# State-space stage of a two-block layer: turned rows in a bank of their own, first z product at the end of the projection

## The chip, the core and the metric

The kernel runs on one core of a Trainium2 chip. A core has a matrix engine (TensorE, PE in the rows; its weight loads are PEld), a vector engine (VectorE, DVE), a scalar engine (ScalarE, ACT), GpSimd (POOL), and SyncE (SP), which here only issues DMAs. Matmul results land in PSUM, eight banks of 128 partitions x 512 fp32. The metric is the device time of one execution in microseconds (us); lower is better, and the figure compared is the median of several runs.

## What is computed

Two transformer-like layers over 512 tokens of width 1024, all in fp32. The first has two branches on one modulated, normalised input `h`: sparse attention and a Mamba-2 state-space branch. The second has banded attention, a gated delta rule and a product-key expert layer. The change touches only the state-space branch, cut here to what matters:

```python
proj = h @ w_in                                   # z_ssm (2048), xbc (3072), dt_raw (32) among it
xbc = silu(causal_depthwise_conv(xbc, conv_w, conv_b))
xs, bm, cm = split(xbc, [2048, 2048 + 512])       # 32 heads of 64; 4 groups of B and C, state 128
dt = softplus(dt_raw + dt_bias); a = -exp(a_log)
y = ssd(xs, dt, a, bm, cm) + d_skip * xs          # chunked scan over 4 chunks of 128 tokens
y = y * silu(z_ssm)
y = rms_norm(y per group of 512 columns) * ssm_norm_g
y_ssm = y @ w_branch_ssm
```

## The kernel before

The program is a row of stages. Each opens a block in which every engine runs its own instruction list; a block ends in a meeting of all engines, so the next stage begins when the last of them is through. Inside a block engines order themselves by semaphores. `post` increments a semaphore and then makes the issuing engine wait for it.

Weights stream from DRAM through a ring of three 2 MB slots. `stream` (SP) issues the loads up to two chunks past the stage's last; `take` (TensorE) waits until a chunk is loaded.

**`ssm_projection_stage`.** TensorE makes 25 products of 8 matmuls (one for dt, 24 for the columns of xbc) into banks 0 to 7 in turn. For each, ScalarE scales and adds the bias (L1061), VectorE adds three further convolution taps (L1099, three instructions), and ScalarE applies silu (L1065, for the last one L1067). `pj.freed` counts banks given back by VectorE; product 23 is the last in bank 7, product 24 is in bank 0.

**`ssd_stage`.** The work is 16 units `n`: 4 groups `g` by 4 chunks `c`, one unit after the other. For each unit:

- `z_product(n)` (L1204): 128 tokens of `h` times 512 columns of the z weights, 8 matmuls of 128x512 in fp32, which the profile shows as 16 passes, into bank 7. ScalarE's `silu_z(n)` (L1284) reads bank 7.
- `front(n)`: TensorE turns the rows of xs and B (L1217, L1218) and multiplies C by B (L1219) into banks 0 and 1. ScalarE copies them out (L1291, L1295) and takes exponentials of the decays (L1297, L1298). VectorE takes the decays, which SP has spread over the partitions by a DMA from DRAM (L1188), and prepares and weights them (L1353 to L1366). GpSimd makes the skip term (L1417) and the decayed rows (L1421).
- `products(n)`: TensorE multiplies everything together (L1233 to L1239), banks 2, 3 and 6. Then GpSimd fades the state (L1428), VectorE updates it and sums the output rows (`sums`, L1377 to L1384), GpSimd multiplies by silu(z) (`gate`, L1433), ScalarE takes the root of the mean square (`root`, L1306 to L1308), and VectorE makes a diagonal matrix of it (`norm`, L1390).
- `turn_back(n)` (L1250): TensorE multiplies the rows of y by that diagonal, 4 matmuls of 128x128, 8 passes, which turns and normalises them, also into bank 7. ScalarE's `store(n)` (L1314) copies them out with the gain.

The order on each engine is written out by hand. On TensorE, iteration `n` is `front(n+1)`, `turn_back(n-2)`, `products(n)`, `z_product(n+2)`; the last two iterations have no z product, and two turn-backs stand behind the loop. On ScalarE it is `front(n+1)`, `store(n-2)`, `root(n-1)`, `silu_z(n+2)`. On VectorE it is `front(n+1)`, `sums(n)`, `norm(n-1)`.

Bank 7 is shared. So `z_product(n)` waits for `silu_z(n-1)` and `store(n-4)`, and `turn_back(n)` waits for `silu_z(n+3)` beside its own `norm(n)` and `store(n-1)`. Before the loop, TensorE turns dt and its cumulative sums into bank 4 (L1255, L1256), from which ScalarE copies three small tiles (L1321 to L1323); TensorE waits for these before `z_product(0)`, and nothing else uses bank 4.

`ssm_out_stage` follows, and then the second block.

Of the kernel before, what the change touches and what calls it, by code (L numbers as in the profile page):

```python
# [1014 lines left out]
def ssm_projection_stage(k, t):  # L1015
# [3 lines left out]
    with ExitStack() as ctx:  # L1019
# [9 lines left out]
        dt_plan = columns(find(k, "w_in", DT0, 32), k.hT)  # L1029
        plan = dt_plan + columns(find(k, "w_in", XBC0, 3072), k.hT)  # L1030
        pj = Projection(k, ctx, "ssm_in", plan)
        first_tap = Signal(ctx, nc, "conv_first_tap")
        convolved = Signal(ctx, nc, "convolved")
        absed = Signal(ctx, nc, "dt_minus_abs")
# [9 lines left out]
        @block.tensor  # L1044
        def _(pe):
            pj.run(pe)

        @block.scalar
        def _(act):
# [58 lines left out]
def ssd_stage(k, t):  # L1108
# [4 lines left out]
    with ExitStack() as ctx:  # L1113
# [21 lines left out]
        ss = sb("group_squares", [P, 2])  # L1135
        diag = sb("rstd_diagonal", [P, 2, P])
        z_chunks = find(k, "w_in", ZS0, 2048)
        z_made = ctx.enter_context(nc.semaphore("z_product"))
        z_in = Signal(ctx, nc, "silu_z_ready")
        smalls = ctx.enter_context(nc.semaphore("dt_acum_turned"))  # L1140
        small_in = Signal(ctx, nc, "dt_acum_rows")
# [52 lines left out]
        def _(pe):  # L1194
            def z_product(n):
                g, c = units[n]
                w = k.take(pe, z_chunks[g])
                if n > 0:
                    pe.wait_ge(z_in.sem, n)
                if n > 3:  # L1200

                    pe.wait_ge(stored.sem, n - 3)
                for kk in range(KD):
                    last = pe.matmul(k.bank[7][:], k.hT[:, kk, c * P:(c + 1) * P], w[:, kk, :],  # L1204
                                     start=(kk == 0), stop=(kk == KD - 1))
                sem, _ = z_there(n)
                last.then_inc(sem, 1)
                k.used.n += c == NT - 1
# [33 lines left out]
            def turn_back(n):  # L1242

                pe.wait_ge(normed.sem, n + 1)

                pe.wait_ge(z_in.sem, min(n + 4, len(units)))
                if n > 0:
                    pe.wait_ge(stored.sem, n)
                for j in range(4):
                    last = pe.matmul(k.bank[7][:, j * P:(j + 1) * P], y[:, n % 2, j * P:(j + 1) * P],  # L1250
                                     diag[:, n % 2, :], start=True, stop=True)
                last.then_inc(back, 1)

# [2 lines left out]
                last = pe.transpose(k.bank[4][:, c * 64 + SH:c * 64 + 64], t.acumT[:, c * P:(c + 1) * P],  # L1256
                                    k.const("ident", SH, SH))
            last.then_inc(smalls, 1)
            pe.wait_ge(small_in.sem, 2)
            z_product(0)  # L1260
            front(0)
            z_product(1)
            for n in range(len(units)):
                if n < last_unit:
                    front(n + 1)
                if n > 1:
                    turn_back(n - 2)
                products(n)
                if n + 2 <= last_unit:
                    z_product(n + 2)  # L1270
# [4 lines left out]
        def _(act):  # L1275
# [34 lines left out]
            def store(n):  # L1310
                g, c = units[n]
                act.wait_ge(back, n + 1)
                for j in range(4):
                    ins = act.activation(t.xbcT[:, 4 * g + j, c * P:(c + 1) * P], k.bank[7][:, j * P:(j + 1) * P],  # L1314
                                         ACT.Copy, scale=k.col("ssm_norm_g", 4 * g + j))
                    if j == 3:
                        post(act, ins, stored)
# [171 lines left out]
def ssm_branch(k):  # L1489
    with ExitStack() as ctx:  # L1490
        def sb(name, shape):
            return ctx.enter_context(k.nc.sbuf_tensor(name, shape, F32))

        t = Part()
        t.xbcT = sb("xbcT", [P, 24, T])
        t.dtT, t.acumT = sb("dtT", [SH, T]), sb("acumT", [SH, T])
        t.acum_scratch = k.nc.dram_tensor("acum_scratch", (SH, T), F32, kind="Internal").ap()
        ssm_projection_stage(k, t)
        ssd_stage(k, t)
        ssm_out_stage(k, t)  # L1500
# [1898 lines left out]
```

## Time and profile before

| | |
|---|---|
| median of 3 runs | 3014.27 us (3012.93 to 3036.82) |
| the profiled execution's own time | 3013.47 us |
| its span in the profile | 3011.7 us |
| TensorE busy | 2635.2 us, 87% of the span |
| VectorE, ScalarE, GpSimd busy | 1659.2, 795.4, 1151.4 us |
| mean DMA rate | 235 GB/s |

The profile shows one execution. Times in its rows are in microseconds from the start of the span. A row of the timeline gives the start, the length, the engine, the line of the kernel, the operation, what it writes and reads, how many instructions were merged, and in brackets how long the engine was idle before it and what ended the idleness. Matmuls overlap, so the next row may start before the length of the last has run out.

### The profile page before, as it was taken

Reading aid. Unit: us, or ns where it says so; the run is one execution under the profiler, and the core shown is the slowest. Engines: PE = TensorE matmul, PEld = TensorE weight load, DVE = VectorE, ACT = ScalarE, POOL = GpSimd, SP = SyncE. Lnnn points to the kernel's source line nnn.
Section 4 is the critical chain, followed back from the end, with each engine's and each line's share of the span. In section 5 each row is a group of like instructions: output and inputs, shape, how many; then the busy total and the mean of one; then the engine's idle time right before and its main releaser. Section 6 shows DMA issues by size and latency. Waiting matters only on the chain. (4 is left out here: it accounts for less than half of the span.)

```text
span 3011.7 us, 26054 instructions
## 1 busy us (share of the span) xinstructions
PE 2635.2 (87%) x8398; PEld 1379.1 (46%) x8398; DVE 1659.2 (55%) x3647; ACT 795.4 (26%) x1616; POOL 1151.4 (38%) x1091
## 2 busy tenths in 40 slices
PE   7999899988979989998799989969987687767877
PEld 3444444445544435577684555636533233222322
DVE  2057824335420124355269998766677777777764
ACT  2013312237750002232224323222222112212121
POOL 0000000012210000000037767666777777777775
PEclk8999999999989999999899989989999999999999
DMA  7226103122212104221269989999999999999998
GB/s 305 74 112 278 57 30 112 65 76 64 63 70 84 56 28 167 99 84 63 102 205 358 340 317 358 395 352 355 349 405 407 395 409 403 404 404 402 409 409 350
DMA packets 185462, 709.01 MB, mean 235 GB/s; under 512 B 20416, under 2 KB 43344, under 8 KB 175216
## 3 DMA queue, kind: packets, MB, share of 16 engines
q0 software_dynamic: 147456, 536.94, 46.2%
q1 hardware_dynamic: 37584, 169.45, 15.1%
q8 instruction: 68, 1.11, 0.2%
q10 hardware_dynamic: 288, 0.96, 0.1%
q14 instruction: 66, 0.54, 0.1%
HBM read 703.01 MB, written 4.27 MB: 235 GB/s over the span
## 5 line engine op out<-in xcount | busy, mean ns | idle before, releaser
L3189 PE MATMUL bank<-ring,xT 128*128 128x512 f32 x1516 | 765.1, 643 | 179.0 <-ACT xT L3165 79.6
L3072 DVE CUSTOM_DVE_ANT_0 ring<-ring,second_arena 128x1024 f32<-128x1024 f32 x380 | 465.7, 1226 | 217.2 <-DMA ring<-in_peer_expert_down,experts 171.4
L3189 PEld LDWEIGHTS bank<-ring,xT 128*128 128x128 f32 x1516 | 293.4, 204 | 589.2 <-issue 377.1
L2997 POOL DMA_INDIRECT ring<-in_peer_expert_down,experts x380 | 410.2, 1080 | 131.3 <-issue 114.4
L2997 POOL DMA_INDIRECT ring<-in_peer_expert_up,experts x384 | 394.9, 1028 | 160.7 <-issue 101.3
L488 PE MATMUL bank<-hT,ring 128*128 128x512 f32 (+2 forms) x1168 | 435.8, 533 | 6.4 <-DMA ring<-in_weights 1.9
L488 PEld LDWEIGHTS bank<-hT,ring 128*128 128x128 f32 (+1 forms) x1168 | 223.5, 194 | 211.9 <-issue 200.4
L2997 POOL DMA_INDIRECT second_arena<-in_peer_expert_down,experts x132 | 141.9, 1075 | 440.0 <-DVE experts L3055 395.6
L1417 POOL TENSOR_TENSOR xs_skip<-xs_rows,rows 128x512 f32<-128x512 f32 x16 | 16.7, 1042 | 765.2 <-ACT xs_rows L1295 647.1
L3165 ACT ACTIVATE xT<-consts,expert_coefs 128x128 f32<-128x128 f32 x505 | 177.9, 394 | 407.5 <-PE bank L3189 274.5
L3189 PE MATMUL bank<-second_arena,xT 128*128 128x512 f32 x504 | 239.7, 607 | 23.5 <-DMA second_arena<-in_peer_expert_up,experts 23.5
L486 PE MATMUL bank<-ring,hT 128*128 128x512 f32 (+1 forms) x512 | 215.7, 578 | 0.9 <-PEq L255 0.9
L3072 DVE CUSTOM_DVE_ANT_0 second_arena<-second_arena 128x1024 f32<-128x1024 f32 x132 | 161.7, 1225 | 44.9 <-DMA second_arena<-in_peer_expert_down,experts 42.2
L3189 PEld LDWEIGHTS bank<-second_arena,xT 128*128 128x128 f32 x504 | 91.8, 191 | 148.0 <-issue 89.2
L2997 POOL DMA_INDIRECT second_arena<-in_peer_expert_up,experts x128 | 130.1, 1016 | 56.1 <-issue 34.9
L486 PEld LDWEIGHTS bank<-ring,hT 128*128 128x128 f32 x512 | 96.6, 192 | 106.8 <-issue 101.7
L3156 ACT ACT_TABLE_LOAD x31 | 39.8, 1283 | 341.4 <-DVE expert_dots L3072 341.1
L1204 PE MATMUL bank<-ring,hT 128*128 128x512 f32 x256 | 115.6, 605 | 3.6 <-ACT exp_acum_rows L1323 2.3
L1099 DVE SCALAR_TENSOR_TENSOR xbcT<-bank,cols,xbcT 128x511 f32<-128x511 f32 (+2 forms) x72 | 53.9, 749 | 102.5 <-ACT xbcT L1061 100.7
L488 PE MATMUL bank<-xbcT,ring 128*128 128x512 f32 x256 | 110.0, 592 | 0.0
L488 PE MATMUL bank<-hT,second_arena 128*128 128x256 f32 x384 | 93.2, 386 | 13.6 <-SPq L1546 12.3
L388 POOL TENSOR_TENSOR hT<-xT,norm_rstd 128x512 f32<-128x512 f32 x3 | 5.1, 1733 | 248.9 <-DVE norm_rstd L379 248.9
(525 smaller groups left out, 3109.7 us busy)
## 6 DMA issues: line engine op xcount, KB each, us to landing
ring<-in_weights SPq DMA_DIRECT2D x65, 2048.0 KB, 8.1
second_arena<-in_weights SPq DMA_DIRECT2D x12, 1024.0 KB, 8.6
decay<-acum_scratch SPq DMA_DIRECT2D x16, 512.0 KB, 5.2
ring<-in_peer_expert_up,experts POOLq DMA_INDIRECT x384, 7.0
ring<-in_peer_expert_down,experts POOLq DMA_INDIRECT x380, 6.9
second_arena<-in_peer_expert_down,experts POOLq DMA_INDIRECT x132, 6.7
x_rows<-in_x SPq DMA_DIRECT2D x1, 2048.0 KB, 12.0
x_rows_scratch<-second_arena SPq DMA_DIRECT2D x2, 1024.0 KB, 8.7
```

The lines of the kernel that those rows point to most:

```text
L388: pool.tensor_tensor(k.hT[:, i, :], k.xT[:, i, :], rstd[:], ALU.mult).then_inc(scaled_p.sem, 1)
L486: last = pe.matmul(held[i][:, 0:n], fixed[:, kk, i * P:(i + 1) * P], w[:, kk, 0:n], **flags)
L488: last = pe.matmul(held[i][0:wide, 0:self.width], w[:, kk, i * P:i * P + wide], fixed[:, which * ring.depth + kk, :], **flags)
L1099: ins = dve.scalar_tensor_tensor(t.xbcT[:, j, back:T], bank[:, 0:T - back], k.col("conv_w", (3 - back) * 24 + j), t.xbcT[:, j, back:T], AL ...
L1204: last = pe.matmul(k.bank[7][:], k.hT[:, kk, c * P:(c + 1) * P], w[:, kk, :], start=(kk == 0), stop=(kk == KD - 1))
L1417: pool.tensor_tensor(skip[:], x3, bc(k.row("d_skip")[:, hs], 2, tall), ALU.mult)
L2997: pool.indirect_dma_start(out=slot[seat[n]], out_offset=None, in_=d[f"peer_expert_{kind}_2"], in_offset=bass.IndirectOffsetOnAxis(ap=exper ...
L3072: post(dve, dve.tensor_tensor_reduce(row, row, h_row(i), 1.0, 0.0, ALU.mult, ALU.add, dots[:, u % 2, s:s + 1]), dotted)
L3156: post(act, act.activation(dots[:, u % 2, :], dots[:, u % 2, :], ACT.Gelu), gelued)
L3165: act.activation(diag[n % DR], k.const("ident"), ACT.Copy, scale=coef[:, u % 2, s:s + 1]).then_inc(diag_ok.sem, 1)
L3189: last = pe.matmul(k.bank[half][:], diag[n % DR], row[:, half * 512:(half + 1) * 512], start=(h == 0 and s == 0), stop=(h == RH - 1 and s ...
```

## The change

The turned-back rows go to bank 4 and no longer to bank 7. So `z_product` no longer waits for `stored`, and `turn_back` no longer waits for `z_in`. The first z product is made by TensorE at the end of `ssm_projection_stage`, in bank 7, once that bank is free; its semaphore moves to the object that both stages share. In the second stage `front(0)` and `z_product(1)` now stand ahead of TensorE's wait for the small copies out of bank 4.

```diff
--- before.py
+++ after.py
@@ -1029,6 +1029,7 @@
         dt_plan = columns(find(k, "w_in", DT0, 32), k.hT)
         plan = dt_plan + columns(find(k, "w_in", XBC0, 3072), k.hT)
         pj = Projection(k, ctx, "ssm_in", plan)
+        z_chunk = find(k, "w_in", ZS0, 2048)[0]
         first_tap = Signal(ctx, nc, "conv_first_tap")
         convolved = Signal(ctx, nc, "convolved")
         absed = Signal(ctx, nc, "dt_minus_abs")
@@ -1044,6 +1045,12 @@
         @block.tensor
         def _(pe):
             pj.run(pe)
+            w = k.take(pe, z_chunk)
+
+            pe.wait_ge(pj.freed.sem, 24)
+            for kk in range(KD):
+                last = pe.matmul(k.bank[7][:], k.hT[:, kk, 0:P], w[:, kk, :], start=(kk == 0), stop=(kk == KD - 1))
+            last.then_inc(t.z_made, 1)
 
         @block.scalar
         def _(act):
@@ -1135,7 +1142,7 @@
         ss = sb("group_squares", [P, 2])
         diag = sb("rstd_diagonal", [P, 2, P])
         z_chunks = find(k, "w_in", ZS0, 2048)
-        z_made = ctx.enter_context(nc.semaphore("z_product"))
+        z_made = t.z_made
         z_in = Signal(ctx, nc, "silu_z_ready")
         smalls = ctx.enter_context(nc.semaphore("dt_acum_turned"))
         small_in = Signal(ctx, nc, "dt_acum_rows")
@@ -1197,9 +1204,6 @@
                 w = k.take(pe, z_chunks[g])
                 if n > 0:
                     pe.wait_ge(z_in.sem, n)
-                if n > 3:
-
-                    pe.wait_ge(stored.sem, n - 3)
                 for kk in range(KD):
                     last = pe.matmul(k.bank[7][:], k.hT[:, kk, c * P:(c + 1) * P], w[:, kk, :],
                                      start=(kk == 0), stop=(kk == KD - 1))
@@ -1243,11 +1247,10 @@
 
                 pe.wait_ge(normed.sem, n + 1)
 
-                pe.wait_ge(z_in.sem, min(n + 4, len(units)))
                 if n > 0:
                     pe.wait_ge(stored.sem, n)
                 for j in range(4):
-                    last = pe.matmul(k.bank[7][:, j * P:(j + 1) * P], y[:, n % 2, j * P:(j + 1) * P],
+                    last = pe.matmul(k.bank[4][:, j * P:(j + 1) * P], y[:, n % 2, j * P:(j + 1) * P],
                                      diag[:, n % 2, :], start=True, stop=True)
                 last.then_inc(back, 1)
 
@@ -1256,10 +1259,10 @@
                 last = pe.transpose(k.bank[4][:, c * 64 + SH:c * 64 + 64], t.acumT[:, c * P:(c + 1) * P],
                                     k.const("ident", SH, SH))
             last.then_inc(smalls, 1)
-            pe.wait_ge(small_in.sem, 2)
-            z_product(0)
             front(0)
             z_product(1)
+
+            pe.wait_ge(small_in.sem, 2)
             for n in range(len(units)):
                 if n < last_unit:
                     front(n + 1)
@@ -1311,7 +1314,7 @@
                 g, c = units[n]
                 act.wait_ge(back, n + 1)
                 for j in range(4):
-                    ins = act.activation(t.xbcT[:, 4 * g + j, c * P:(c + 1) * P], k.bank[7][:, j * P:(j + 1) * P],
+                    ins = act.activation(t.xbcT[:, 4 * g + j, c * P:(c + 1) * P], k.bank[4][:, j * P:(j + 1) * P],
                                          ACT.Copy, scale=k.col("ssm_norm_g", 4 * g + j))
                     if j == 3:
                         post(act, ins, stored)
@@ -1495,6 +1498,7 @@
         t.xbcT = sb("xbcT", [P, 24, T])
         t.dtT, t.acumT = sb("dtT", [SH, T]), sb("acumT", [SH, T])
         t.acum_scratch = k.nc.dram_tensor("acum_scratch", (SH, T), F32, kind="Internal").ap()
+        t.z_made = ctx.enter_context(k.nc.semaphore("z_product"))
         ssm_projection_stage(k, t)
         ssd_stage(k, t)
         ssm_out_stage(k, t)
```

## Rows read from the trace of the kernel before

**Rows 1.** Engines by stretch: stretch, length, busy time of each, TensorE's granted clock, DMA.
```profile
634.00:645.00 11.00, 10.56 (x22) 4.84 (x23) 2.48 (x11) 0.78 (x3) 0.00 (x0) 0.71 0.72 253
679.00:852.00 173.00, 157.55 (x636) 91.89 (x636) 85.18 (x209) 122.73 (x205) 49.53 (x45) 1.00 0.22 69
```

**Rows 2.** Timeline of TensorE over units 0 to 4.
```profile
658.70 7.03 PE L1204 MATMUL bank<-ring,hT 128*128 128x512 f32 x16
...
669.84 1.02 PE L1239 MATMUL bank<-xs_dt_decay,b_rows 128*128 128x512 f32 x2
670.70 7.03 PE L1204 MATMUL bank<-ring,hT 128*128 128x512 f32 x16
...
678.11 0.39 PE L1219 MATMUL bank<-xbcT 128*128 128x128 f32 x2
...
685.18 7.03 PE L1204 MATMUL bank<-ring,hT 128*128 128x512 f32 x16
...
692.59 0.39 PE L1219 MATMUL bank<-xbcT 128*128 128x128 f32 x2
694.27 1.13 PE L1250 MATMUL bank<-rstd_diagonal,y_rows 128*128 128x128 f32 x8 [1.29 <-issue]
695.23 1.02 PE L1233 MATMUL bank<-xs_skip,consts 128*128 128x512 f32 x2
...
699.60 7.03 PE L1204 MATMUL bank<-ring,hT 128*128 128x512 f32 x16
```

**Rows 3.** Waits from 629 to 900: who waited for whom, total us, times, longest.
```profile
PE bank L1250 <- issue: 15.5, 12, 1.3
...
PE bank L1250 <- ACT silu_z_rows L1284: 1.3, 1, 1.3
```

**Rows 4.** Timeline of ScalarE in the same unit as rows 2's wait.
```profile
693.57 0.60 ACT L1284 ACTIVATE silu_z_rows<-bank 128x512 f32<-128x512 f32 x1
...
697.75 1.14 ACT L1314 ACTIVATE xbcT<-bank,cols 128x128 f32<-128x128 f32 x4
```

**Rows 5.** Timeline of VectorE, unit 2's decays and unit 0's norm.
```profile
671.36 1.80 DVE L1366 TENSOR_TENSOR decay<-decay,cb_causal 128x1024 f32<-128x1024 f32 x1 [1.73 <-ACT decay L1298]
...
677.48 0.29 DVE L1390 TENSOR_SCALAR rstd_diagonal<-consts,group_squares 128x128 f32<-128x128 f32 x1
```

**Rows 6.** Two lines by themselves, VectorE's and GpSimd's: ns min/median/max.
```profile
L1366 DVE TENSOR_TENSOR decay<-decay,cb_causal x16: 1224/1225/1803, 650.1 to 856.5; 128x1024 f32<-128x1024 f32 x16
...
L1421 POOL TENSOR_TENSOR xs_dt_decay<-xs_dt,end_decays x16: 1041/1042/2081, 650.2 to 859.6; 128x512 f32<-128x512 f32 x16
```

**Rows 7.** Timeline of TensorE from the projection's end to products(0).
```profile
617.48 9.18 PE L488 MATMUL bank<-hT,ring 128*128 128x512 f32 x21
631.14 0.28 PE L1255 MATMUL bank<-consts,dtT 32*128 32x32 f32 x1 [4.49 <-PEq L1019]
...
634.44 10.07 PE L1204 MATMUL bank<-ring,hT 128*128 128x512 f32 x16 [2.27 <-ACT exp_acum_rows L1323]
...
654.34 1.02 PE L1233 MATMUL bank<-xs_skip,consts 128*128 128x512 f32 x2
```

**Rows 8.** Timelines of ScalarE, VectorE and GpSimd over the same stretch.
```profile
630.04 0.63 ACT L1067 ACTIVATE xbcT<-xbcT 128x512 f32<-128x512 f32 x1 [1.85 <-DVE xbcT L1099]
...
634.11 0.28 ACT L1323 ACTIVATE exp_acum_rows<-bank 128x128 f32<-128x128 f32 x1
...
647.44 1.28 ACT L1297 ACT_TABLE_LOAD   x1
...
641.35 0.17 DVE L1353 COPY end_decays<-decay 128x8 f32<-128x8 f32 x1 [6.31 <-DMA decay<-acum_scratch]
...
641.75 1.66 DVE L1357 TENSOR_SCALAR decay<-decay,acum_rows 128x128 f32<-128x128 f32 x8
...
650.18 2.08 POOL L1421 TENSOR_TENSOR xs_dt_decay<-xs_dt,end_decays 128x512 f32<-128x512 f32 x1 [1.64 <-ACT decay L1298]
```

**Rows 9.** Timeline of TensorE, first turn-back of the tail.
```profile
864.37 2.07 PE L1250 MATMUL bank<-rstd_diagonal,y_rows 128*128 128x128 f32 x8 [5.98 <-DVE rstd_diagonal L1390]
```

## The prediction

> **What bounds the kernel now.** I read the page first: TensorE is busy 87% of the span, so a stage is worth what its TensorE idles or runs slowly. Then the engines by stretch, to see the stage that the change edits [rows 1]: from 679 to 852 us TensorE is busy 157.55 of 173 us at a granted clock of 1.00 (2.4 GHz), while VectorE works 85 us, ScalarE 123 and GpSimd 50. So TensorE paces the state-space stage, with some 15 us of holes.
>
> The timeline of TensorE shows where the holes are [rows 2]. From one z product to the next it is 699.60 - 685.18 = 14.42 us. In that round there is one hole, ahead of the turn-back: L1219 starts at 692.59, the turn-back (L1250) only at 694.27. The list of waits counts it [rows 3]: 12 times "issue", 15.5 us, and once ScalarE's L1284, 1.3 us, 13 holes in all. "Issue" says that the profile names nobody; the timeline of ScalarE does [rows 4]: silu_z (L1284) ends at 693.57 + 0.60 = 694.17, and the turn-back starts 0.10 us later. That is the wait on `z_in`: bank 7 still holds the z product that ended only before `front`. The same rows show that the other bank wait costs nothing: the store (L1314) ends at 697.75 + 1.14 = 698.89, ahead of the z product at 699.60.
>
> The third place is the start of the stage [rows 7]. TensorE's last projection pass ends at 617.48 + 9.18 = 626.66, but the stage begins at 631.14, after the last silu (630.04 + 0.63 = 630.67 [rows 8]). Then TensorE waits for three small copies until 634.44 and makes the first z product in 10.07 us instead of 7.03; the granted clock from 634 to 645 is 0.71 [rows 1], so part of it ran at the lower level, 1.2 GHz, after an idle stretch. From 626.66 to 644.5 this one product is all the large work that TensorE does.
>
> **The loop, with the bank of its own.** The edit removes `z_in` from 13 turn-backs, those of iterations 2 to 14. What is the round without the hole? Iteration 1 has no turn-back and no hole: 670.70 - 658.70 = 12.00 us [rows 2]. The turn-back itself takes 695.23 - 694.27 = 0.96 us. So the new round is 12.96 us, if TensorE stays the bound, against 14.42: 1.46 us each, 13 x 1.46 = 19.0 us.
>
> It stays the bound only if nothing else that the turn-back and `products` wait for is late. The next in line is `norm` (L1390), which is behind GpSimd's three operations and VectorE's sums, all counted from the end of the preceding products. In iteration 1, the nearest to the new rhythm, products end at 669.84 + 1.02 = 670.86 and norm at 677.48 + 0.29 = 677.77 [rows 2, 5], 6.9 us later. TensorE is through with the z product and front at 678.11 + 0.39 = 678.50, 7.6 us after the products; call it 7.5, since passes overlap. The slack is 0.6 us. It is thin, but it is a repeated distance: both ends count from the same products, and the z product that lies between them is unchanged. The bounds of this term are 19.0 us, and 0 if norm took the whole hole back.
>
> Others in the loop: ScalarE's list per unit starts from the end of the z product, has room (123 of 173 us busy), and keeps its order. The stored wait goes at no gain, as read above. Bank 4 is written only by turn-backs after the small copies, and its reader, `store`, is the same engine and length. `small_in` waits later, by which time it is long past. DMAs in the loop are issued by SP on `multiplied`; they move with the products. No instruction is added in the loop.
>
> Here a rule bears on the slack. GpSimd's L1421 takes 1.04 us in the median and up to 2.08, and that VectorE's L1366 takes 1.22 and up to 1.80 [rows 6]; the 1.80 is in iteration 1, where products ended half a microsecond before it [rows 2, 5]. The Trainium skill, SBUF — State Buffer, "Who interferes with whom", says that a VectorE instruction with two SBUF inputs contends with a GpSimd instruction that reads SBUF, and that whichever begins first holds the shared ports for its whole length. The trace agrees as far as the two long lengths go. By that rule the turn-back, which pushes the end of products 0.96 us later than in iteration 1, lets L1366 go first and delays GpSimd by the rest of one operation, less than the 1.04 us already inside the 6.9; so by the rule rival C below could not come about, and its 0.13 would go to the forecast. No row shows that order of the two, so I leave the chances as they are worked out without it.
>
> **The start.** The first z product moves under the projection's tail. Bank 7 is free since product 23 was convolved, while TensorE was still in product 24, and its weights were requested two chunks ahead, so it starts at once: 626.66 + 6.9 = 633.5 (16 passes at full clock, the 7.03 of rows 2). But the block ends with a meeting of all engines, which was at 630.67 + 0.47 = 631.14. Now TensorE is last, so the meeting is at about 633.5 + 0.5 = 634.0: everything else in the stage, SP's DMAs too, begins 2.9 us later. If TensorE did not hold the others, the shift would be 0.
>
> What is then late? The spread decays. They landed at 641.35 [rows 8]; behind the same DMAs they land at 644.25. VectorE's preparation takes 641.75 + 1.66 - 641.35 = 2.06 us, to 646.3. ScalarE was held before by the z product (its table load for the exponential at 647.44 came after silu_z and the copies); now silu_z(0) is done by 634.39 + 2.9 + 1.28 + 0.60 = 639.2, and it waits for VectorE. From that table load to the end of GpSimd's L1421 it is 650.18 + 2.08 - 647.44 = 4.82 us, so unit 0 is ready at 646.3 + 4.8 = 651.2, and products(0), at 654.34 before [rows 7], start at about 651.3. That is 3.0 us earlier. z_product(1) begins at 639.3 and lasts 7.0 to 10.1 us, so it ends by 649.4 and is hidden either way. The bounds: no z product on the path and no shift gives 5.9 us; a low clock afterwards gives 0. The second is real, since TensorE may idle up to 5 us before products(0), and what followed the idle stretch before cost 10.07 - 7.03 = 3.04 us. I take 3.0: z_product(1) itself comes after a pause of 3 us with only small matmuls before it, so it is likely the slow one, as the first z product was, and then the pause after it is under 2 us.
>
> **The end.** The last iteration's turn-back waits 5.98 us for norm [rows 9], with no z product to cover it, and the low clock follows. That chain counts from the last products, so it moves with them and neither gains nor loses. The later stages are untouched: they start from a meeting of engines and keep their length.
>
> **The sum.** 19.0 + 3.0 = 22.0 us. Against the profiled execution's own time, 3013.47, that leaves 3013.5 - 22.0 = 2991.5 us; its span of 3011.7 becomes 2989.7, with 1.8 us around it as before. The profiled execution lies 0.8 us under the median of the runs shown, 3014.27, which is less than any term here. A difference of 1% is 30.1 us, about what a measurement of this kernel can tell from no change; the forecast of 0.7% is within it.
>
> **The rivals.**
> - B, the start gives nothing. The low clock falls between z_product(1) and products(0) and costs the 3.04 us. For it: the clock was low after the gaps around 631 [rows 1, 7]. Against: the slow product is more likely hidden. 3013.5 - 19.0 = 2994.5 us.
> - C, norm becomes the bound. One more GpSimd operation per unit is held back by VectorE, 1.04 us against a slack of 0.6: the round is 13.4 us, 13 x 1.02 + 3.0 = 16.3 us, 2997.2 us. With two more held back, it overruns by 1.48 and the loop gains nothing: 3013.5 - 3.0 = 3010.5 us. For it: the slack is thin. Against: iteration 1 had the contention and kept its 12.00 us.
> - D, the meeting does not hold SP back, or less: gain at the start 5.9, total 24.9, 2988.6 us.
> - E, slower than before: the low clock enters the loop, because the new rhythm's small gaps now fall beside small matmuls only, and each z product pays the 3.04 us of the first. That decides from 22.0 / 3.04 = 7.2, so 8 or more of the 13 rounds; with all 13 it is 39.5 - 22.0 = 17.5 us slower, 3031.0 us. Against: through 13 rounds with a hole each, the clock stayed at 1.00 [rows 1], and there will be fewer holes.
>
> **How the numbers follow.** The forecast has a chance of 0.62; B 0.18; C 0.10 with one operation and 0.03 with two; D 0.04; E 0.03. The predicted time is 2991.5 us. The range from 2987 to 3003 takes in D, B, the first C and, for unequal rounds, part of the way to the second; it leaves out the second C, E and stray measurements. Faster by over 1% (under 2984.1) is in no case but a larger one that I have not found, 0.03; slower by over 1% needs E and more, 0.03; within 1%, 0.94.
>
> **What would show it right or wrong.** Right: TensorE's z products 12.96 us apart in iterations 2 to 14, no idle row on L1250 until the tail; one z product on the projection's line at 626.5; the stage's first instruction at 634.0; products(0) at 651.3; norm ending about 0.6 us before the turn-back. Wrong: an idle before L1250 with "rstd_diagonal L1390" behind it (C); a granted clock of under 1.00 between 651 and 665 (B), or between 665 and 850 (E); the first decays landing at 641 (D); TensorE's z product at the projection's end starting late, because its bank or weights were not there.

## The result, and the profile after

The changed kernel took 3000.64 us (median of 6 runs, 2994.11 to 3005.59) against 3014.77 us for the kernel before (6 runs). The ratio of the comparison is 0.9937, with a 95% interval of 0.9908 to 0.9966; the two medians by themselves give 0.9953, which lies inside it. The forecast was 2991.5 us, a ratio of 0.992, and a range of 2987 to 3003: faster, by less than 1%, and so it is. The profiled execution took 2994.11 us with a span of 2992.3, against 3011.7 before.

The timeline of TensorE in the changed kernel, over two rounds, answers to [rows 2]. A row gives start, length, engine, line and operation as before.

```profile
679.41 7.03 PE L1208 MATMUL bank<-ring,hT 128*128 128x512 f32 x16
...
686.82 0.39 PE L1223 MATMUL bank<-xbcT 128*128 128x128 f32 x2
687.05 1.06 PE L1253 MATMUL bank<-rstd_diagonal,y_rows 128*128 128x128 f32 x8
687.94 1.02 PE L1237 MATMUL bank<-xs_skip,consts 128*128 128x512 f32 x2
...
692.30 7.03 PE L1208 MATMUL bank<-ring,hT 128*128 128x512 f32 x16
```

The hole is gone: the turn-back starts 0.23 us after L1223's start instead of 1.68, and the z products are 692.30 - 679.41 = 12.89 us apart instead of 14.42. The engines by stretch say the same for the whole loop, beside [rows 1]: TensorE is busy in all of 130 us, and the clock stays up.

```profile
634.00:645.00 11.00, 7.65 (x17) 3.50 (x16) 2.45 (x11) 4.59 (x7) 1.04 (x1) 0.69 0.84 287
645.00:651.00 6.00, 4.29 (x15) 2.04 (x14) 4.01 (x11) 5.17 (x7) 2.08 (x1) 1.00 0.00 0
700.00:830.00 130.00, 130.00 (x540) 76.88 (x540) 70.44 (x166) 103.46 (x172) 46.89 (x38) 1.00 0.28 85
```

In the list of waits, which answers to [rows 3], three waits of the turn-back are left, all in the tail:

```profile
PE bank L1253 <- DVE rstd_diagonal L1393: 9.0, 2, 6.5
...
PE bank L1253 <- ACT xbcT L1317: 4.7, 1, 4.7
```

The start of the stage on TensorE answers to [rows 7]:

```profile
616.64 9.18 PE L488 MATMUL bank<-hT,ring 128*128 128x512 f32 x21
625.65 7.03 PE L1052 MATMUL bank<-ring,hT 128*128 128x512 f32 x16
633.00 0.21 PE L1258 MATMUL bank<-consts,dtT 32*128 32x32 f32 x1 [0.32 <-PEq L1019]
...
637.92 9.55 PE L1208 MATMUL bank<-ring,hT 128*128 128x512 f32 x16 [3.35 <-ACT silu_z_rows L1287]
...
650.08 1.10 PE L1237 MATMUL bank<-xs_skip,consts 128*128 128x512 f32 x2
```

The projection ends at 625.82. The early z product follows without a pause at full clock, the stage begins 7.2 us after the projection (4.5 before), the second z product is the slow one, and products(0) stand 24.3 us after the projection instead of 27.7.

**Where the time went.** Totals are a poor ruler here, stages a good one. I measure the *stretch*: from the end of TensorE's last projection pass to the first matmul of the stage after. It was 884.78 - 626.66 = 258.1 us and is 860.60 - 625.81 = 234.8, so 23.3 us less: 3.4 at the start, 19.8 between products(0) and products(14) (199.5 to 179.7), 0.1 in the tail. The span fell by only 19.4. The expert stage, which nobody touched, took 8.4 us of it back: from TensorE's last projection matmul to the end of the span it was 3011.7 - 2126.7 = 885.0 us before and 2992.3 - 2098.9 = 893.4 after. The other 4.5 us between the two were gained in stages that are the same code in both, 0.8 ahead of the stretch and 3.6 between it and the expert stage. In the ten executions of the first table below, the expert stage, the same code each time, takes between 884 and 903 us, and between 884 and 898 in four of them on one and the same chip. So experiments are judged by their stretches, and single totals are told but not weighed.

### The profile page after: what moved, and what is told of

Read it like the earlier page. It is cut to its first block, busy times and chain, and to the rows that moved or that the text cites. A ratio compares the mean times of both kernels' runs of the same rounds, so it can differ in the third digit from the quotient of the medians.

```text
span 2992.3 us, 26054 instructions
## 1 busy us (share of the span) xinstructions
PE 2625.3 (88%) x8398; PEld 1372.6 (46%) x8398; DVE 1659.1 (55%) x3647; ACT 795.6 (27%) x1616; POOL 1169.9 (39%) x1091
## 3 DMA queue, kind: packets, MB, share of 16 engines
q1 hardware_dynamic: 37584, 169.45, 15.2%
## 4 chain that ended last, share of the span: by engine, by line
PE 22%; POOL 14%; issue 7%; DMA 5%; DVE 3%; ACT 0%; POOLq 0%; SPq 0%; DVEq 0%; ACTq 0%
PE bank L3193 14%; POOL ring L3001 11%; PE bank L488 4%; DMA ring<-in_peer_expert_down,experts 3%; POOL second_arena L3001 3%; DVE ring L3076 1%; PE bank L2035 0%; DMA second_arena<-in_peer_expert_down,experts 0%; DMA ring<-in_peer_expert_up,experts 0%; DMA x_rows_scratch<-second_arena 0%; DMA out<-xT 0%; PE bank L2012 0%; PE bank L2329 0%; PE bank L2336 0%; PE bank L2334 0%
## 5 line engine op out<-in xcount | busy, mean ns | idle before, releaser
L3001 POOL DMA_INDIRECT ring<-in_peer_expert_up,experts x384 | 412.5, 1074 | 159.0 <-issue 96.7
L3001 POOL DMA_INDIRECT ring<-in_peer_expert_down,experts x380 | 402.4, 1059 | 131.3 <-issue 114.3
L1420 POOL TENSOR_TENSOR xs_skip<-xs_rows,rows 128x512 f32<-128x512 f32 x16 | 24.7, 1546 | 727.4 <-ACT xs_rows L1298 638.3
L3193 PE MATMUL bank<-second_arena,xT 128*128 128x512 f32 x504 | 239.2, 607 | 22.5 <-DMA second_arena<-in_peer_expert_up,experts 22.4
L3001 POOL DMA_INDIRECT second_arena<-in_peer_expert_up,experts x128 | 136.4, 1066 | 56.3 <-issue 33.3
L1208 PE MATMUL bank<-ring,hT 128*128 128x512 f32 x240 | 108.0, 603 | 3.3 <-ACT silu_z_rows L1287 3.3
```

The source lines that it names most:

```text
L1420: pool.tensor_tensor(skip[:], x3, bc(k.row("d_skip")[:, hs], 2, tall), ALU.mult)
L3001: pool.indirect_dma_start(out=slot[seat[n]], out_offset=None, in_=d[f"peer_expert_{kind}_2"], in_offset=bass.IndirectOffsetOnAxis(ap=exper ...
L3193: last = pe.matmul(k.bank[half][:], diag[n % DR], row[:, half * 512:(half + 1) * 512], start=(h == 0 and s == 0), stop=(h == RH - 1 and s ...
```

## The experiments

In the table, *start* is from the projection's end to products(0), *loop* from products(0) to products(14), *tail* from products(14) to the next stage; us of one profiled execution each.

| kernel | total, single or median | start | loop | tail | stretch |
|---|---|---|---|---|---|
| before | 3013.47 | 27.7 | 199.5 | 30.9 | 258.1 |
| changed | 2994.11 | 24.3 | 179.7 | 30.8 | 234.8 |
| bank and waits alone | 3001.96 | 27.7 | 179.6 | 30.9 | 238.2 |
| early z product alone | 3032.16 | 24.6 | 199.6 | 30.8 | 255.1 |
| changed, wait for silu put back | 3021.57 | 24.4 | 199.6 | 33.1 | 257.1 |
| changed, wait for store put back | 3016.90 | 24.4 | 192.5 | 31.2 | 248.1 |
| changed, skip made twice | 2995.38 | 25.4 | 185.7 | 33.1 | 244.1 |
| changed, spreads first | 2991.51 | 22.3 | 179.7 | 31.8 | 233.8 |
| changed, first z product split | 2999.55 | 22.4 | 180.3 | 31.4 | 234.1 |
| changed, tail in another order | 3000.65 | 24.4 | 179.7 | 32.5 | 236.5 |

The first four experiments ran on one chip, the kernel before taking 3005.90 us there in a single run, the next four on a second, with 3018.87. Four more kernels ran on a third, where the expert stage alone took 971 to 981 us (kernel before there: 3118.41, median of 17 runs):

| kernel | total | start | loop | tail | stretch |
|---|---|---|---|---|---|
| changed, skip made thrice | 3104.42 | 24.8 | 200.1 | 34.2 | 259.1 |
| changed, both edits of the start | 3089.44 | 19.8 | 179.7 | 31.3 | 230.7 |
| the same with idle matmuls in the tail | 3084.21 | 19.8 | 179.7 | 28.2 | 227.7 |
| changed, again | 3093.02 | 25.6 | 180.4 | 31.5 | 237.5 |

**The two halves of the change.** First the bank alone:

```diff
-            w = k.take(pe, z_chunk)
-
-            pe.wait_ge(pj.freed.sem, 24)
-            for kk in range(KD):
-                last = pe.matmul(k.bank[7][:], k.hT[:, kk, 0:P], w[:, kk, :], start=(kk == 0), stop=(kk == KD - 1))
-            last.then_inc(t.z_made, 1)
...
+            pe.wait_ge(small_in.sem, 2)
+            z_product(0)
             front(0)
             z_product(1)
-
-            pe.wait_ge(small_in.sem, 2)
```

> The bank and its two waits alone; the first z product is back at the start of the state-space stage. Measured from the end of TensorE's last projection pass to the first matmul of the stage after, the kernel before has 258.1 us and the changed one 234.8. My theory: the round between z products is 12.89 us with no hole before the turn-back, the start is as before, so 13 rounds give some 19.9 us: 238.2 us. Rival (the rounds only got shorter because the start shifted the engines against each other): a hole of 0.5 us or more stays before the turn-backs, and the stretch is over 244 us.

Measured 238.2 us with the loop at 179.6: the theory to the tenth. Then the early product alone, with the rows in bank 7 and both waits back:

```diff
+                if n > 3:
+                    pe.wait_ge(stored.sem, n - 3)
...
+                pe.wait_ge(z_in.sem, min(n + 4, len(units)))
...
-                    last = pe.matmul(k.bank[4][:, j * P:(j + 1) * P], y[:, n % 2, j * P:(j + 1) * P],
+                    last = pe.matmul(k.bank[7][:, j * P:(j + 1) * P], y[:, n % 2, j * P:(j + 1) * P],
...
-                    ins = act.activation(t.xbcT[:, 4 * g + j, c * P:(c + 1) * P], k.bank[4][:, j * P:(j + 1) * P],
+                    ins = act.activation(t.xbcT[:, 4 * g + j, c * P:(c + 1) * P], k.bank[7][:, j * P:(j + 1) * P],
```

> The early z product alone; the turned rows are in bank 7 again with both waits. My theory: rounds of 14.42 us as before with the hole of 1.29 us, and only the start is shorter, by the 3.4 us that the changed kernel's trace shows beyond the 0.8 us it had already gained earlier: stretch 258.1 - 3.4 = 254.7 us. Rival (the start gives nothing by itself): 258 us.

Measured 255.1, rounds of 14.42. The two halves bring 19.9 and 3.0 us alone, and 23.3 together: they add up within 0.4 us. `front(0)` and `z_product(1)` stay ahead of the wait for the small copies in this second kernel, as in the change; what that order gives without the early product was not measured.

**The wait or the bank?** The wait for silu alone is put back, with the rows still in bank 4:

```diff
                 pe.wait_ge(normed.sem, n + 1)
+                pe.wait_ge(z_in.sem, min(n + 4, len(units)))
```

> The changed kernel with the turn-back's wait for silu of z put back, though its bank is another. My theory (the wait is what cost, not the bank): rounds of 14.42 us again, stretch 234.8 + 13 x 1.5 = 254.7 us. Rival (sharing the bank made accesses slow in itself, and the wait was cheap): rounds near 12.9 us, stretch near 235 us.

The loop is 199.6 us again: all of the loop's gain is in this wait, none in the bank as such. The wait is one for ScalarE's silu, and its rows show what it is made of. The z product ends at 741.44 + 7.03 = 748.47; ScalarE loads a table, takes silu until 750.44, and the turn-back starts 0.09 us later:

```profile
748.54 1.28 ACT L1287 ACT_TABLE_LOAD   x1 [3.93 <-issue]
749.84 0.60 ACT L1287 ACTIVATE silu_z_rows<-bank 128x512 f32<-128x512 f32 x1
```
```profile
750.53 1.13 PE L1253 MATMUL bank<-rstd_diagonal,y_rows 128*128 128x128 f32 x8 [1.29 <-issue]
```

So 1.28 of the 1.97 us from the z product's end to silu's end are the table load. Whether an earlier load would have shortened the hole without a second bank was not tried.

The stretch is 2.4 us over what was expected, 2.3 of it in the tail, where this execution made products(15) at the lower clock for longer:

```profile
862.95 2.08 PE L1253 MATMUL bank<-rstd_diagonal,y_rows 128*128 128x128 f32 x8 [5.98 <-DVE rstd_diagonal L1393]
864.82 1.91 PE L1237 MATMUL bank<-xs_skip,consts 128*128 128x512 f32 x2
866.52 3.52 PE L1240 MATMUL bank<-xs_dt,decay 128*128 128x64 f32 x16
```

L1240 takes 3.52 us here and 1.90 at the same place of the changed kernel.

**The wait that I had at nothing.** The wait for the store is put back:

```diff
                 if n > 0:
                     pe.wait_ge(z_in.sem, n)
+                if n > 3:
+                    pe.wait_ge(stored.sem, n - 3)
```

> The changed kernel with the z product's wait for the store of an older unit put back. My theory: the store ends before TensorE comes to it, so nothing changes: rounds of 12.89 us, stretch 234.8 us within 0.3. Rival (in the shorter round the store is late, ScalarE having a longer list): rounds longer by some tenths of a us, stretch over 238 us.

It is the rival that came true, and by more than its tenths of a us: rounds are 13.94 us and the loop is 12.8 us longer, a stretch of 248.1 us. TensorE, then ScalarE, in one of these rounds:

```profile
751.34 1.02 PE L1245 MATMUL bank<-xs_dt_decay,b_rows 128*128 128x512 f32 x2
753.17 7.11 PE L1210 MATMUL bank<-ring,hT 128*128 128x512 f32 x16 [0.81 <-ACT xbcT L1319]
```
```profile
747.70 0.60 ACT L1289 ACTIVATE silu_z_rows<-bank 128x512 f32<-128x512 f32 x1
...
751.88 1.14 ACT L1319 ACTIVATE xbcT<-bank,cols 128x128 f32<-128x128 f32 x4
```

ScalarE turns to silu when the last z product has ended, works without a pause from there, and ends the store 4.7 us behind silu, at 753.02: the store is fixed by the z product and not by the turn-back. In the old round TensorE came to its next z product 0.71 us after the store [rows 2, 4]. In the new one it comes 1.53 us earlier and would be too early. The changed kernel shows the same without the wait: its store, below, ends at 680.49, 1.08 us after the z product began at 679.41; from iteration 5 on it is 0.83 us.

```profile
679.35 1.14 ACT L1317 ACTIVATE xbcT<-bank,cols 128x128 f32<-128x128 f32 x4
```

The wait was free only behind the other. Had only the wait for silu been taken away, 12.8 of the loop's 19.8 us, two thirds, would not have come.

**How much room norm has.** GpSimd's skip product is made twice, then three times, which puts 1.1 us each between products and norm:

```diff
+                p(pool.tensor_tensor(skip[:], x3, bc(k.row("d_skip")[:, hs], 2, tall), ALU.mult))
                 pool.tensor_tensor(skip[:], x3, bc(k.row("d_skip")[:, hs], 2, tall), ALU.mult)
```

> The changed kernel with GpSimd's skip product (1.04 us, about 1.1 with its wait) made twice in each unit; it lies between the end of the products and norm. In the changed kernel's trace norm ends 1.03 us before the turn-back in the steady rounds. My theory (norm is next in line, with that slack): rounds of 12.9 to 13.1 us, an idle of at most 0.2 us before the turn-back. If the 0.6 us of the prediction were the slack, rounds of 13.4 us. Rival (something else, ScalarE or a DMA, is next): rounds stay at 12.89 with the slack of norm not used up. Stretch 235 to 237.5 us by the theory.

> The changed kernel with GpSimd's skip product made three times in each unit: some 2.2 us more between the end of the products and norm. With it made twice, rounds were 12.9 to 13.5 us and the holes before the turn-back 0.33. My theory (norm is next in line with about 1 us of slack in most rounds): rounds of 14.0 to 14.6 us, in most of them an idle before the turn-back of 1 us or more that ends with norm; the gain of the bank is gone. Rival (another wait takes over and GpSimd stays hidden): rounds under 13.7 us.

Twice gave rounds of 12.89 to 13.84 us, the most frequent 13.48, and a hole ahead of seven turn-backs, 0.68 us once and 0.32 or 0.33 otherwise, so norm is next in line. After the first round, 13 rounds grew by 5.2 us together, 0.40 each; my 12.9 to 13.1 was too low for half of the rounds, and the stretch, 244.1 us, lies far over my 235 to 237.5 (1.1 of it in the start, 2.3 in the tail). The 0.40 is a mean of unlike rounds: about 0.59 in six, 0.95 in one, 0.23 in three, and nothing in the three at a group's end. The trace shows why 1.1 us did not fit into 1.03 of room: the first of the two skips now begins ahead of VectorE's decay product (L1369), which takes 2.04 us in such a round and 1.23 in the changed kernel, and the second skip takes 1.90 instead of 1.04. Three times gave three rounds in four of 14.24 to 14.96 and the fourth, at a group's end where the state is not faded, of 12.9; the 13 rounds grew by 16.4 us, 1.26 each, and the stretch, 259.1, is within 1 us of that of the kernel before. TensorE with the skip made three times:

```profile
783.00 1.02 PE L1243 MATMUL bank<-xs_dt_decay,b_rows 128*128 128x512 f32 x2
...
793.11 1.16 PE L1253 MATMUL bank<-rstd_diagonal,y_rows 128*128 128x128 f32 x8 [1.45 <-DVE rstd_diagonal L1393]
```

The hole names its cause this time. The room itself is read in the changed kernel, from VectorE's norm to TensorE's turn-back, in iterations 2 and 3 and in a steady round:

```profile
673.30 0.29 DVE L1393 TENSOR_SCALAR rstd_diagonal<-consts,group_squares 128x128 f32<-128x128 f32 x1
...
686.33 0.29 DVE L1393 TENSOR_SCALAR rstd_diagonal<-consts,group_squares 128x128 f32<-128x128 f32 x1
...
827.55 0.29 DVE L1393 TENSOR_SCALAR rstd_diagonal<-consts,group_squares 128x128 f32<-128x128 f32 x1
```
```profile
674.15 1.06 PE L1253 MATMUL bank<-rstd_diagonal,y_rows 128*128 128x128 f32 x8
...
828.87 1.06 PE L1253 MATMUL bank<-rstd_diagonal,y_rows 128*128 128x128 f32 x8
```

That is 0.56 us in iteration 2, 687.05 - 686.62 = 0.43 in iteration 3, and 1.03 in the steady round. The prediction's 0.6 was read for the same norm as that of iteration 2, unit 0's. At a group's end the state is not faded and the room is larger, 2.16 us in iteration 4.

**The start.** Two experiments, each on one link of its chain. SP's weight load goes behind the first two spreads:

```diff
-            k.stream(sp, z_chunks[0])
             sp.wait_ge(scratch_in, 16)
...
                 sp.dma_start(dec[:, n % 2], spread).then_inc(bcast[n % 2], 16)
+                if n == 1:
+                    k.stream(sp, z_chunks[0])
```

> The changed kernel with SP's 2 MB weight load put behind the first two spreads of decays. The first spread landed 8.3 us after its issue behind that load, 5.2 in the median alone. My theory (that landing sets the start): decays 3.1 us earlier; the second z product, made at the low clock, then becomes the bound, so products(0) start 1.5 to 2.0 us earlier, at 22.3 to 22.8 us after the projection instead of 24.3; stretch 233.0. Rival (TensorE's slow second z product sets it already): no change, 234.8.

VectorE's row shows the landing; the spread had been issued at 636.92:

```profile
643.34 0.17 DVE L1357 COPY end_decays<-decay 128x8 f32<-128x8 f32 x1 [4.49 <-DMA decay<-acum_scratch]
```

That is 15.2 us after the projection's end instead of 17.1: 1.9 us earlier, not 3.1, since the spread took 6.4 us to land where I had counted on the median's 5.2. products(0) come at 22.3 us, as expected, and now TensorE is the bound: front(1) follows its slow z product without an idle row. The stretch is 233.8 us where 233.0 was expected; the tail of this execution is 0.9 us longer. Then the first z product is split:

```diff
-            for kk in range(KD):
-                last = pe.matmul(k.bank[7][:], k.hT[:, kk, 0:P], w[:, kk, :], start=(kk == 0), stop=(kk == KD - 1))
-            last.then_inc(t.z_made, 1)
+            for kk in range(4):
+                pe.matmul(k.bank[7][:], k.hT[:, kk, 0:P], w[:, kk, :], start=(kk == 0), stop=False)
...
+            w = k.take(pe, z_chunks[0])
+            for kk in range(4, KD):
+                last = pe.matmul(k.bank[7][:], k.hT[:, kk, 0:P], w[:, kk, :], start=False, stop=(kk == KD - 1))
+            last.then_inc(z_made, 1)
```

> The changed kernel with only half of the first z product (4 of 8 matmuls, 3.4 us) at the end of the projection and the rest at the start of the next stage, so that TensorE is not last at the meeting. My theory (the meeting held everything back by 2.7 us): the stage starts 4.5 us after the projection instead of 7.2, and products(0) 2.7 us earlier, at 21.6; stretch 232.1 us. Rival (TensorE's own work is the path, whoever is late): the stage starts earlier but products(0) stay at 24.3 us; stretch 234.8.

The stage starts 4.5 us after the projection, as expected, and products(0) 1.9 us earlier, not 2.7: TensorE idled 2.85 us ahead of front(1), and front and the first product ran at the lower clock.

```profile
636.55 7.11 PE L1207 MATMUL bank<-ring,hT 128*128 128x512 f32 x16 [1.35 <-ACT silu_z_rows L1290]
646.50 1.09 PE L1220 MATMUL bank<-consts,xbcT 128*128 128x128 f32 x4 [2.85 <-DVE decay L1372]
...
648.02 1.75 PE L1236 MATMUL bank<-xs_skip,consts 128*128 128x512 f32 x2
```

L1220's 1.09 us are 0.63 in the changed kernel, L1236's 1.75 are 1.10. Both edits together:

> The changed kernel with both edits of the start: half of the first z product at the end of the projection, and the decays' first two spreads ahead of the weight load. Each alone brought products(0) from 24.3 to 22.3 us after the projection. My theory (the landing of the decays is the path in both, and TensorE's clock stays up if its pauses are short): products(0) at 18.5 to 20 us, stretch 229.5 to 231 us. Rival (each hides the other's gain behind TensorE's second z product): 22 us and 234. In the total a gain of 4 us against the changed kernel is inside what one execution differs from the next; the ratio to the kernel before should be near 0.992.

products(0) come at 19.8 us, 4.5 us before the changed kernel's, and the wait before front(1) is 0.89 us. The gains of the two (2.0 and 1.9) add up and 0.6 more comes on top. The granted clock from 645 to 651 is 1.00 here and 0.72 with the split alone, which fits my theory that the clock stays up through the short pause; no run separates the clock from the rest.

**The tail.** Its three pauses (6.5, 2.6, 4.7 us) looked like a matter of order:

```diff
+            store(last_unit - 1)
             root(last_unit)
-            store(last_unit - 1)
             store(last_unit)
...
+                if n >= last_unit - 1:
+                    norm(n - 1)
                 sums(n)
-                if n > 0:
+                if 0 < n < last_unit - 1:
                     norm(n - 1)
```

> The changed kernel with its tail rewritten: VectorE makes the last norms ahead of the sums of the next unit, and ScalarE stores unit 14 ahead of the last root. My theory (the 6.5, 2.6 and 4.7 us of idle in the tail come from the order of the lists, not from the data): the first goes down by 1.5 to 2 us, the last by about 1; tail from products(14) 28 us instead of 30.8, stretch 232 us. Rival (the chain of data, products, sums, gate, root, norm, sets it): 30.8 us still.

The tail got 1.6 us longer. The first pause shrank from 6.48 to 4.97 us and the second went away, but the last grew from 4.72 to 6.70, where I had expected 1 us less, and all of products(15) ran at the lower clock:

```profile
845.61 2.08 PE L1253 MATMUL bank<-rstd_diagonal,y_rows 128*128 128x128 f32 x8 [4.97 <-DVE rstd_diagonal L1393]
847.98 2.05 PE L1237 MATMUL bank<-xs_skip,consts 128*128 128x512 f32 x2 [0.29 <-DVE y_rows L1387]
849.82 3.51 PE L1240 MATMUL bank<-xs_dt,decay 128*128 128x64 f32 x16
```

Neither theory is tested cleanly by this, because the clock moved along with the order. So the clock was tried by itself, with matmuls that nobody reads (5, 2 and 4 of them) in the three pauses, on top of both edits of the start:

```diff
+            def filler(count):
+                for _ in range(count):
+                    pe.matmul(k.bank[5][:], k.const("ident"), k.hT[:, 0, :], start=True, stop=True)
...
+                if n == last_unit:
+                    filler(5)
...
+            filler(2)
             turn_back(last_unit - 1)
+            filler(4)
             turn_back(last_unit)
```

> As the kernel with both edits of the start, and 11 matmuls of 128x512 without use (each two passes of 0.43 us) in the three idle places of TensorE's tail, 5, 2 and 4 of them, into bank 5 that the stage doesn't use. My theory (the low clock costs the tail and the first product of the next stage): the clock stays at 1.00, the tail from products(14) is 28 us instead of 30.8, and the next stage's first 128 passes take 55.2 us instead of 57.1, together some 4 to 5 us. Rival (the fillers only delay what comes behind them, or the tail is bound by the other engines' chain): the tail is 30 to 32 us.

The tail is 28.2 us, against 31.3 in the same kernel without these matmuls and 30.8 to 33.1 in every other kernel with the tail's order unchanged and one skip, and the next stage's first product took 55.0 us instead of 57.3, both as expected. TensorE with the filler, and then the whole tail from products(14) on, with the filler and without:

```profile
833.28 4.45 PE L1248 MATMUL bank<-hT,consts 128*128 128x512 f32 x10
839.92 1.16 PE L1257 MATMUL bank<-rstd_diagonal,y_rows 128*128 128x128 f32 x8 [2.19 <-DVE rstd_diagonal L1405]
...
841.78 1.89 PE L1240 MATMUL bank<-xs_dt,decay 128*128 128x64 f32 x16
```
```profile
828.92:857.15 28.23, 21.78 (x92) 12.46 (x91) 8.02 (x18) 19.84 (x41) 6.21 (x5) 1.00 0.05 21
```
```profile
825.51:856.80 31.29, 15.40 (x70) 10.84 (x69) 8.03 (x18) 19.84 (x41) 6.21 (x5) 0.75 0.05 22
```

The granted clock is 1.00 against 0.75, and the first turn-back of the tail takes 1.16 us against 2.08. ScalarE and GpSimd are busy for the same time in both. Last, the changed kernel again, for totals on the same chip:

> The changed kernel itself, for a comparison of totals on the same chip as the two others and a second trace. Stretch 234.8 us give or take 1, rounds of 12.89; the total about 15 to 20 us under the kernel before.

Its stretch is 237.5 us, 2.7 over the first trace's and outside the 1 us that I gave it. Of the excess 2.1 us lie in the start and the first round (1.3 and 0.8) and are rival B's: the clock fell ahead of front(1), after z_product(1) had already been slow, and from 645 to 651 it is 0.75 where the first trace has 1.00. The other 0.6 us lie in the tail.

```profile
636.28 9.55 PE L1208 MATMUL bank<-ring,hT 128*128 128x512 f32 x16 [3.35 <-ACT silu_z_rows L1287]
648.26 1.08 PE L1221 MATMUL bank<-consts,xbcT 128*128 128x128 f32 x4 [2.44 <-DVE decay L1369]
...
649.78 1.85 PE L1237 MATMUL bank<-xs_skip,consts 128*128 128x512 f32 x2
```

The ratios to the kernel before, on that chip: 0.9929 (0.9907 to 0.9950) for the changed kernel, 0.9919 (0.9896 to 0.9942) with both edits of the start, 0.9907 (0.9879 to 0.9934) with the idle matmuls too. The intervals overlap, so the totals alone don't rank the three. The parts do: with filler the stretch and the next stage's first product are 227.7 + 55.0 = 282.7 us, against 230.7 + 57.3 = 288.0 with both edits of the start alone, and 234.8 + 57.1 = 291.9 and 237.5 + 57.4 = 294.9 in the two traces of the changed kernel. Each of these sums is one execution.

## Why the prediction was right, and where it was not

- **The hole.** Right in place, cause and size. 13 turn-backs lost it, the round fell by 1.53 us where 1.46 was taken (the turn-back costs 0.89 and not 0.96 once it follows without a pause), 19.8 us in the loop against 19.0. The wait put back brings it all back.
- **"The stored wait goes at no gain, as read above."** This step failed. It was read in the old round, where the store ended 0.71 us before TensorE came; the change shortens that round by 1.5. The prediction's own rows had it: 699.60 - 1.46 = 698.14, ahead of the store's end at 698.89. Put back, the wait costs 1.04 us a round, 12.8 us in all. The sum was not hurt, since the change removes it, but the reason given was wrong, and a reader who kept that wait as harmless would have lost two thirds of the loop's gain.
- **"It stays the bound."** Right. The slack of 0.6 us holds for iteration 2 (0.56); iteration 3 has 0.43 and the steady rounds 1.03. Rival C did not happen, though norm is the next bound. Its prices, 0.44 and 1.48 us a round for one and two GpSimd operations of 1.04 us, lie near the 0.40 and 1.26 measured with one and two more skips, but that is in part luck: the steady rounds have more slack than was taken, and the added skip also lengthens VectorE's decay product.
- **The start.** The chain was right link by link: the stage began 7.2 us after the projection (forecast 7.3), the decays set it, the slow z product was the second and was hidden. 3.0 us were forecast, 3.4 came in the one trace and 2.1 in the other, where the clock fell once more as rival B had it and the first round cost 0.8 more. Six traces have this start: five at 24.3 to 24.6 us after the projection, this one at 25.6. B and the forecast are thus two outcomes of one kernel. Rival D, a meeting that doesn't hold SP back, is refuted: the split product moved the stage's start by 2.7 us and the decays' landing by 2.5 (640.29 - 625.66 against 642.96 - 625.81).
- **The tail.** Moved and unchanged, as said (30.9 and 30.8). Filling its pauses brought 3.1 us, and 2.3 more in the next stage, with the clock at 1.00; the prediction had not looked for that.
- **Rival E**, the low clock in the loop: no. From 700 to 830 the clock is 1.00.
- **The total.** 22.0 us were forecast; the stretch gave 23.3, the profiled execution 19.4, the medians 14.1. The step from 23.3 to 19.4 is unchanged code, the expert stage above all, which differed by up to 14 us between executions on one chip, and by 19 over the ten; what makes it differ was not tried. For the step from 19.4 to 14.1 there is no trace: the profiled execution was the fastest of its six. The median, 3000.64 us, lies 9.1 us over the forecast and past rival B's 2994.5, so the total by itself doesn't tell forecast from rival. That it lies in the range owes to the range's width; the sum is borne out by the stretch.

The rule on the shared ports (the Trainium skill, SBUF — State Buffer, "Who interferes with whom") can now be read with VectorE first in the rounds of the loop. The prediction says that no row shows that order, which is not quite so: in unit 0 of the kernel before VectorE's L1366 begins at 650.14 and keeps its 1.23 us, and GpSimd's L1421, begun at 650.18 [rows 8], takes 2.08. In iteration 3 of the changed kernel VectorE's decay product begins first and is not lengthened (1.23 us), and GpSimd's skip, begun 0.33 us later, takes 1.80 us instead of 1.04:

```profile
679.42 1.23 DVE L1369 TENSOR_TENSOR decay<-decay,cb_causal 128x1024 f32<-128x1024 f32 x1 [1.85 <-ACT decay L1301]
```
```profile
679.75 1.80 POOL L1420 TENSOR_TENSOR xs_skip<-xs_rows,rows 128x512 f32<-128x512 f32 x1 [5.03 <-PE bank L1243]
```

VectorE is done at 680.65 and GpSimd at 681.55, 0.90 us later, close to the whole 1.04 us of an undisturbed skip. By that rule the first to begin holds the ports for its whole length; the trace agrees. The prediction's use of it came out so far as the order goes: with the turn-back in the round VectorE does begin first, from iteration 3 on, and GpSimd's two operations together end sooner, 2.80 us after the first began in iteration 3 and 2.55 in the steady rounds against 3.03 in iteration 2. It doesn't explain the slack by itself, which is smallest in iteration 3.

## What to carry to other kernels

Price every wait that a change removes in the new rhythm, not in the old: a wait that ends 0.7 us early is free only until the round is 0.7 us shorter, and here the two waits on one bank had to go together. When work is moved ahead of a meeting of all engines, look at how much of it the others' tail covers: here the part that stuck out held the next stage's first DMA back by 2.7 us. Where totals vary by more than the effect, measure the edited stage between two fixed instructions in the trace.

## What was not expected of the hardware

The granted clock in the start and the tail was not the same from one execution to the next: two executions of the changed kernel differ by 2.1 us in the start and the first round, and tails of one and the same order take from 30.8 to 33.1 us. In products(15), L1240 took 1.90 and 2.47 us in two executions of the changed kernel, and 3.52 with the wait for silu put back. Eleven matmuls without use (22 passes) took about 9.9 us of TensorE's idle time (4.45, 1.88 and 3.60), the clock stayed at 1.00, and the same kernel gained 3.1 us in the tail and 2.3 us in the stage behind it, in one execution of each.
